# Two transformer blocks on one core: rotary key projected four column groups at a time, low-rank RMS factors moved into later steps, modulation chunks placed elsewhere

## The reference

```python
q = rms_norm(rms_norm(a_q, q_a_norm) @ w_uq, q_norm)        # 256 -> 16 heads x 96
ckv = rms_norm(a_kv[..., :128], kv_a_norm); k_pe = a_kv[..., 128:]     # 32 rotary columns
k_nope, v = split(ckv @ w_ukv)                              # per head 64 + 64
k = rms_norm(concat([k_nope, k_pe]), k_norm)                # k_pe shared by the heads
# rotary on the last 32 of q and k (k of the tokens only), softmax(q k / sqrt(96)) v, @ w_o
```

## Time and profile before

| | us |
|---|---|
| median of 3 runs | 3618.05 (3613.52 to 3625.37) |
| the profiled execution | 3612.44 |
| its span on the core | 3610.6 |
| TensorE busy (matmuls) | 3333.5 (92%) |
| VectorE, ScalarE, GpSimd busy | 1522.1, 1336.0, 1319.5 |

### The profile page before, as it was taken

How to read it: one execution, slowest core, us unless ns; L and a number is a source line. 1 busy time by engine, 2 the same in 40 slices (tenths; PEclk the granted TensorE clock), 3 DMA queues, 4 the chain that set the end, 5 groups by cost and what they waited for, 6 DMA issues and landing times.

```text
span 3610.6 us, 40889 instructions
## 1 busy us (share of the span) xinstructions
PE 3333.5 (92%) x16580; PEld 2671.7 (74%) x16580; DVE 1522.1 (42%) x2662; ACT 1336.0 (37%) x2305; POOL 1319.5 (37%) x731
## 2 busy tenths in 40 slices
PE   7988899999967989999989998989998989889998
PEld 4854788888854667788877687868887667768886
DVE  5557332222245776321233546253223455734232
ACT  4222332222323565332333534343333453434243
POOL 2224432222320000544462047444455124564446
PEclk9999999999978999999999999999999999999999
DMA  5145112112104200123222120322322212022322
GB/s 222 59 157 200 47 55 72 56 62 65 58 5 167 74 13 1 70 88 105 85 100 90 41 83 1 108 77 85 108 88 94 70 47 75 6 84 94 105 85 67
DMA packets 85639, 286.11 MB, mean 79 GB/s; under 512 B 9771, under 2 KB 10347, under 8 KB 84940
## 3 DMA queue, kind: packets, MB, share of 16 engines
q1 hardware_dynamic: 85452, 283.50, 23.3%
HBM read 281.37 MB, written 2.10 MB: 79 GB/s over the span
## 4 chain that ended last, share of the span: by engine, by line
PE 81%; DVE 12%; ACT 4%; DMA 1%; issue 1%; POOL 0%; SPq 0%; DVEq 0%; ACTq 0%
PE ps L443 19%; PE ps L446 19%; PE ps L444 19%; PE ps L468 2%; PE ps L470 2%; PE ps L469 2%; PE ps L1847 2%; DMA ring<-in_w_mod 1%; PE ps L1786 1%; DVE T L2397 1%; PE ps L500 1%; DVE T L616 1%; PE ps L1119 1%; DVE sm L1792 1%; PE ps L1820 1%
## 5 line engine op out<-in xcount | busy, mean ns | idle before, releaser
L388 POOL TENSOR_TENSOR WL<-ring,WH 128x1024 fp32r<-128x1024 f32 (+2 forms) x444 | 960.5, 2167 | 1587.0 <-ACT WH L379 1586.4
L443 PE MATMUL ps<-HX,WH 128*128 128x512 f32 x1832 | 719.0, 392 | 3.5 <-POOL WL L388 3.5
L446 PE MATMUL ps<-HX,WL 128*128 128x512 f32 x1832 | 716.2, 391 | 0.0
L444 PE MATMUL ps<-HX,WH 128*128 128x512 f32 x1832 | 714.7, 390 | 0.0
L379 ACT CAST WH<-ring 128x1024 fp32r<-128x1024 f32 (+2 forms) x444 | 420.7, 949 | 450.1 <-PE ps L446 327.6
L443 PEld LDWEIGHTS ps<-HX,WH 128*128 128x128 f32 x1832 | 344.0, 188 | 83.7 <-issue 5.7
L443 PE MATMUL ps<-FR,WH 128*128 128x512 f32 (+1 forms) x1072 | 400.0, 373 | 0.0
L444 PE MATMUL ps<-FR,WH 128*128 128x512 f32 (+1 forms) x1072 | 390.9, 372 | 0.0
L446 PEld LDWEIGHTS ps<-HX,WL 128*128 128x128 f32 x1832 | 345.3, 188 | 51.9
L444 PEld LDWEIGHTS ps<-HX,WH 128*128 128x128 f32 x1832 | 344.3, 188 | 51.1
L446 PE MATMUL ps<-FR,WL 128*128 128x512 f32 (+1 forms) x1072 | 370.6, 372 | 0.0
(11 more groups left out here) (334 smaller groups left out, 5391.5 us busy)
## 6 DMA issues: line engine op xcount, KB each, us to landing
ring<-in_w_mod SPq DMA_DIRECT2D x96, 512.0 KB, 6.1
ring<-in_ffn_w_up SPq DMA_DIRECT2D x88, 512.0 KB, 3.4
ring<-in_w_up SPq DMA_DIRECT2D x88, 512.0 KB, 3.4
ring<-in_w_in_tok SPq DMA_DIRECT2D x40, 512.0 KB, 3.5
ring<-in_w_in_feat SPq DMA_DIRECT2D x32, 512.0 KB, 3.4
ring<-in_ffn_w_down SPq DMA_DIRECT2D x32, 384.0 KB, 3.1
ring<-in_w_out SPq DMA_DIRECT2D x32, 384.0 KB, 3.1
ring<-in_w_down SPq DMA_DIRECT2D x32, 384.0 KB, 3.1
```

The costliest lines, as they stand in the source:

```text
L388: pool.tensor_tensor(WL[:, p % SPLITS, 0:n], ring.ap(r), WH[:, p % SPLITS, 0:n], ALU.subtract).then_inc(*ring.frees(r, split.g, "low", p))
L443: pe.matmul(o, high, xh, k == 0, False)
L444: pe.matmul(o, high, xl, False, False)
L446: m = pe.matmul(PS[bs[i]][:, 0:N], low, get(k)[0], False, k == g.kt - 1)
```

## The change

- **Key.** The key's weights are no longer split. 32 float32 matmuls (weights 32 columns, activations' high and low part as float32, 512 or 256 streamed) write four column groups; ScalarE copies the two banks, six small matmuls with `pick`, now 128 x 32, add the groups and turn them.
- **Low-rank factors.** The gains are applied as ScalarE evicts the low-rank tiles; their squares are summed by one-column matmuls. RMS of q's low-rank part drops out of the head norm but for its eps, which becomes eps times (mean square + eps), a value per token (`epsq`). The reciprocal root of ckv's (`rkv`) is the scale of the key and value evictions. Heads start after the evictions ("low"); the table and the key and value evictions wait for `rkv` ("small").
- **Chunks.** The mixer steps ten (4 to 9, 12 to 15), one less after the transposes and one less between the inverse transforms. Chunks 10 and 11 run in gap n1, 16 and 17 in n2, 22 and 23 in n3, right after the sums; 18 to 21 in the making of head group 0, every third step; none in attention. `PLACE` gives the order for the two row buffers. In the diff `rows_pe` is the eight matmuls of a chunk, `turned_pe` its four with `pick[:, 0:2]`, both as before; `some_a` copies each row by ScalarE once it is complete; VectorE's one addition for both chunks (`some_v`) stands after all its parts.

```diff
+        def some_pe(pe, c0, n):
+            b = bank.take("mod_n", c0)
+            pe.wait_ge(*bank.free("mod_n", c0))
+            for c in range(c0, c0 + n):
+                rows_pe(pe, c)
+                if c > c0:
+                    turned_pe(pe, c - 1, b, 8 * (c - 1 - c0))
+            turned_pe(pe, c, b, 8 * (c - c0))
...
+        def norm_a(act, name, sts, c0, n):
             for q in sts:
                 root_a(act, q.name, q.N, q.r)
+            some_a(act, c0, n, [nm.pe.at("total", q.name) for q in sts])
             parts_a(act, name, sts)
...
+            r = ring.raw(dr["mla_w_kpe"], 256)
+            for i, (N, parts) in enumerate(((S, HX), (SC, HC))):
+                for half in range(2):
+                    for x in range(2):
+                        for j in range(4):
+                            k = 4 * half + j
+                            m = pe.matmul(PS[bs[i]][32 * j:32 * j + 32, 0:N], ring.ap(r)[:, k * 32:k * 32 + 32], parts[:, k, x, :].bitcast(F32),
+                                          half == 0 and x == 0, half == 1 and x == 1)
...
+            for t in range(4):
+                for k in range(2):
+                    pe.matmul(PS[b][:, t:t + 1], sq[:, k, t * 128:t * 128 + 128], ones[:, 0:1], k == 0, k == 1)
             for t in range(6):
+                m = pe.matmul(PS[b][:, 4 + t:5 + t], sq[:, 2 + t // 4, t % 4 * 128:t % 4 * 128 + 128], ones[:, 0:1], True, True)
...
+            for t in range(6):
+                m = pe.matmul(PS[b][:, t * 32:t * 32 + 32], KP[:, t * 128:t * 128 + 128], pick[:, :], True, True)
...
+                    act.activation(sq[:, g.key + s, 0:N], o, ACT.Square).then_inc(*mla.a.up())
+                    act.activation(dst, o, ACT.Identity, scale=gain).then_inc(*bank.emptied((L_a.name, g.key, s), mla.a))
...
+            dve.tensor_scalar(rkv, ps("stat")[:, 4:10], 1.0 / 128, EPS, ALU.mult, ALU.add).then_inc(*mla.v.up("mean kv"))
+            dve.tensor_scalar(epsq, ps("stat")[:, 0:4], EPS / 256, EPS * EPS, ALU.mult, ALU.add).then_inc(
+                *bank.emptied(("stat",), mla.v))
...
+                dve.scalar_tensor_tensor(by_tile, by_tile, 1.0 / w, eps_of, ALU.mult, ALU.add).then_inc(
...
-            pe.wait_ge(*nm.v.at("small"))
+            pe.wait_ge(*mla.a.at("low"))
...
-                act.copy(ktok[:, t, :].rearrange("p (h c) -> p h c", h=4)[:, :, 0:64], kv[:, :, 0:64]).then_inc(
-                    *mla.a.up())
+                act.wait_ge(*mla.v.at("small"))
+                act.activation(ktok[:, t, :].rearrange("p (h c) -> p h c", h=4)[:, :, 0:64], kv[:, :, 0:64], ACT.Identity,
+                               scale=rkv[:, t:t + 1]).then_inc(*mla.a.up())
...
             for x, _ in enumerate(heads(0)):
-                if x % 4 == 2:
+                if x % 3 == 2:
                     next(last_mod, None)
+            last_of(last_mod)
...
             totals_pe(pe, ["n1x", "n1c"])
+            some_pe(pe, 10, 2)
...
-                        sp.wait_ge(*nm.v.at("small"))
+                        sp.wait_ge(*mla.v.at("small"))
```

More of the change, by code:

```diff
@@ L349, in program @@
         L_ffn0 = ffn_plan("ffn0", "ffn_w_up", "ffn_w_down", 0, 2)
[L350 removed]
+        L_a = Linear(ring, "mla_a").rows(dr["mla_w_a"], 0, 3, 8)
         L_o = Linear(ring, "mla_o").rows(dr["mla_w_o"], 0, 8, 8)
@@ L473, in token_pe, with row_of, rows_pe @@
                     next(beside, None)
+        PLACE = {c: i for i, c in enumerate((*range(0, 10), 12, 13, 14, 15, 10, 11, *range(16, 24)))}
+        def row_of(c):
+            return T[:, 6 + PLACE[c] % 2, :]
+        def rows_pe(pe, c):
+            b = bank.take("mod", c)
+            pe.wait_ge(*bank.free("mod", c))
+            for q in range(4):
+                r = ring.raw(dr["w_mod"][c // 12][c % 12][q], 1024)
+                pe.wait_ge(*ring.landed(r))
+                for j in range(2):
+                    k = 2 * q + j
+                    o = PS[b][32 * (k % 4):32 * (k % 4) + 32, :]
+                    m = pe.matmul(o, cs[:, k, :], ring.ap(r)[:, j * 512:j * 512 + 512], k < 4, k >= 4)
+                m.then_inc(*ring.frees(r, mod.pe, "row", c, q))
@@ L543, in scales_v @@
                                          ALU.add, ALU.mult).then_inc(*nm.v.up())
[L545 to L560, removed]
         def first_sums_a(act, name, src, N, r):
@@ L1550, in ready @@
                 return parts_done("n2", sts, s)
-            linear_pe(pe, L_a, lambda g: [(halves[s], (S, SC)[s], ready(s)) for s in range(1 + (g.key == 2))],
-                      groups=L_a.groups[0:3], front=2)
-            g = L_a.groups[3]
-            p = ring.next()
-            pe.wait_ge(*split.g.at("low", p))
-            b = bank.take("kpe")
-            pe.wait_ge(*bank.free("kpe"))
-            for t in range(6):
-                for k in range(8):
-                    src = (HX, HC)[t // 4]
-                    tt = slice((t % 4) * 128, (t % 4) * 128 + 128)
-                    c = slice(k * 32, k * 32 + 32)
-                    o = PS[b][:, t * 32:t * 32 + 32]
-                    pe.matmul(o, src[:, k, 0, tt], WH[:, p % SPLITS, c], k == 0, False)
-                    pe.matmul(o, src[:, k, 0, tt], WL[:, p % SPLITS, c], False, False)
-                    m = pe.matmul(o, src[:, k, 1, tt], WH[:, p % SPLITS, c], False, k == 7)
@@ new lines, in low_rank_a @@
+                    act.activation(dst, o, ACT.Identity, scale=gain).then_inc(*bank.emptied((L_a.name, g.key, s), mla.a))
+                mla.a.mark("low")
+            act.wait_ge(*mla.pe.at("kpe rows"))
+            for i, N in enumerate((S, SC)):
+                act.copy(KP[:, i * S:i * S + N], ps("kpe", i)[:, 0:N]).then_inc(*bank.emptied(("kpe", i), mla.a))
+            mla.a.mark("kpe")
+            cast_to(act, g.last + 3)
+            act.wait_ge(*mla.v.at("mean kv"))
+            act.activation(rkv, rkv, ACT.Sqrt).then_inc(*mla.a.up("root kv"))
```

186 lines of the change are left out of this document (89 added, 97 removed).

## The result

The changed kernel takes 3569.5 us (median of four runs, 3564.5 to 3573.6) against 3617.4 of the kernel before beside it: ratio 0.9864, 95% interval 0.9841 to 0.9887. Measured a second time, the same kernel gave 0.9884 (0.9864 to 0.9905) with a median of 3575.5. The forecast was 3560, within 3540 to 3582. The profiled execution took 3566.0 us (span 3564.2), 46.4 less than the profiled one before; the sum had said 54.4.

A forecast was written before the change was run, and what follows sets the result against it. TensorE, busy 92% of the span, bounds the kernel. Terms -37.6 - 0.5 + 0.4 + 0.5 - 15.0 + 5.7 - 5.9 - 2.0 = -54.4 give 3558.0 profiled, 3563.6 on the median; forecast 3560 us, range 3540 to 3582.

The forecast's parts named there:

- Low-rank stage: Rotary key and low-rank norms up to the first query matmul: 16.0 us instead of 53.6, gain 37.6 (31 to 39).
- Rival (a): Key matmuls in four column groups don't overlap: 21.4 us instead of 6.5, 3573 on the profiled execution; chance 10%.
- Warmer query matmuls: First query matmuls, 7.38 us before, may be less cold after a shorter idle: 0.5 us gained (0 to 2).
- Evictions: Key and value evictions become scaled activations, 0.12 us more each: +0.4 in head group 0, +0.5 in groups 1 to 3.
- Mixer: Two of twelve chunks leave the mixer: 7.6 us gained at its front, 7.4 at its end, together -15.0.
- The three gaps: Two chunks in each norm gap; late ring slots and ScalarE's row copy delay the modulated parts: +5.7 us (2 to 14).
- The flight: Late chunk transfers in the gaps: a 512 KB transfer lands 3.4 us after issue, the two behind it 1.3 us each.
- rival (b): Late gap transfers take 6.1 us instead of 3.4, 2.7 more in each gap: +8, 3566; chance 15%.
- Attention 0: Four chunks leave the first attention, 85.9 us before and 80.0 without them: gain 5.9 (5 to 7).
- Transposes: The last chunk's rows leave the transposes that end the latent stage: 2.0 us gained (1 to 3.4).
- Rival (c): Work in the gaps keeps TensorE's clock at the high level: 6.5 us more gained, 3551; chance 15%.
- (d): Slower than before: nothing prefetched in the gaps, eight transfers in a row, 40 us per gap, 3672; chance 3%.

The follow-up runs named there:

- chunks_only: Kernel before plus the chunk moves alone, with its old low-rank stage and evictions: 3612.0 us beside 3612.9 of the kernel before.
- lowrank_only: Kernel before plus the low-rank part alone, chunks where they stood before: 3575.0 us beside 3612.9 of the kernel before.
- rope_later: Changed kernel with the rotary table's transfer issued behind the first head group's weights instead of ahead of them: ratio 0.9857 to the kernel before.
- key_split: Changed kernel with the rotary key computed as before (144 matmuls on high and low halves), the RMS folding kept: 3597.6 us, ratio 0.9955 to the kernel before.
- key_serial: Changed kernel with the 32 key matmuls ordered one column group after another instead of in turn: key 11.6 us at full clock instead of 5.3.
- after_again: Changed kernel run once more, unaltered, beside the follow-up runs on the same chip: ratio 0.9884 to the kernel before, median 3575.5 us.
- cap: Changed kernel with the next stage's third weight split named after the eight chunk transfers in the three gaps: 3564.8 us, ratio 0.9854 to the kernel before.
- late_turn: Changed kernel with the second chunk's row copied after all modulated parts and turned after the next stage's first pair: ratio 0.9870 to the kernel before.
- key_wide: Changed kernel with key matmuls in serial order and 128 weight columns each, key not computed, trace only: both halves take 20.6 us.
- best2: Changed kernel with late_turn, rope_later, cap in first and third gap only, and chunk 14's addition after two channels: 3561.3 us, ratio 0.9850 to the kernel before.

## Why the prediction was right, and where it was wrong

The total was right: 3560 forecast, 3569.5 and 3575.5 measured. Of its two parts, measured apart, only the low-rank one was. For the chunk moves the terms of the sum were -15.0 + 5.7 - 5.9 - 2.0 = -17.2, and chunks_only measures a ratio of 0.9992, which is -3 us (-7 to +1). That the total stayed in its range is in part luck: the range was wide enough to hold this miss.

- **Low-rank stage: right.** -37.6 forecast, -39.5 in the trace, -38 by lowrank_only. Key 5.3 (6.5 forecast: the 256-column half took 1.84, half of the other, so its weight loads don't pace it), statistics and turn 4.7 (4.7), the wait that ends the stage 4.2 (0.9 for the chain and 3.9 for the flight; 0.5 and 3.7 measured), and rope_later shows that this wait is SyncE's order. TensorEngine Tiling (Array Packing) of the Trainium skill, section Theoretical Speedup, allows up to four times for 32 columns. Against the wide matmul the runs have 3.8 and 3.7, but the packing alone makes only a factor of 2.2 (11.6 to 5.3), the narrow weights the rest. About half of what the key gained is the lower level that its 144 matmuls ran at (see key_split).
- **Rival (a): fell, and its price was wrong.** It priced matmuls that don't overlap at 21.4 us; key_serial measured 11.6. That step took L1119 as the price of a serial narrow matmul, though it differs in two things, width and order. With 11.6 (a) would have given 3563, well inside the range, so the total could not have told it.
- **Warmer query matmuls: -0.5 forecast, not shown.** From the first query matmul to the first key/value matmul the first trace has 6.76 us instead of 7.22, but after_again, the same kernel, has 8.17, and the twelve traces with the short idle have a mean of 7.23 (6.67 to 8.28). That the first trace met the term is luck.
- **Evictions: right.** 0.47 each for 0.38, less than the 0.50 taken. From the key/value matmuls to the transposes +1.4 in all, 1.2 of it VectorE's wait for chunk 18's turn: there the step that held the waits for rows 19 and 20 to be within 0.2 us failed. What made it late is the clock: the last quarter of the rows took 1.73 us and the turn 1.87, at the lower level. In rope_later that quarter lands 20.2 us after the first query matmul, no sooner than here (19.9), but quarter and turn take 1.05 each, and VectorE does not wait. So it is in all traces: a wait of 1.2 to 1.9 us in the six with both at the lower level, 0.6 in after_again with only the rows there, none in the five others with the chunk order of the change.
- **Mixer: right by the traces' means.** -7.5 at the front and -7.8 at the end where -7.6 and -7.4 stood, though the whole stretch fell by 13.1 only in the first trace. Over the twelve traces with the moved chunks it has a mean of 150.5, against 164.0 and 167.0 in the two without, which is the forecast 15.0, give or take the 3 us between these two. Missed: the stall of up to 2.6 us at the bank which chunk 14's addition frees; the addition is no longer covered by a second chunk.
- **The three gaps: the term that was mis-sized.** +1.3, +1.6, +2.8 forecast, +3.4, +3.7, +4.2 measured: 11.3 instead of 5.7 (10.9 in the mean of the eight traces with the changed kernel's gaps), inside the range of 2 to 14 and no gap over 5. The mechanism was the one named: late slots, and ScalarE's copy ahead of all parts. The forecast took off 0.8 for a TensorE that starts less cold, which no idle time shows, so like for like 6.5 stands against 11.3. Mis-sized were two steps. The flight: the step had a 512 KB transfer land 3.4 us after its issue and the two behind it at 1.3 us each; in the first gap they took 3.5, 4.9 and 7.3 from the first issue, so the last was 1.3 us late. The step from that landing to the first part: 1.0 by the sum, for rows and copy, 1.6 measured (425.00 to 426.59). In the third gap the last transfer was late by 0.4 us only (8.5 after the sums, 8.2 forecast), and the second step was the larger; in the second gap the last rows also ran at a granted clock of 0.60. In size 5.6 us is two thirds of the way to rival (b). That the six transfers right behind are what delayed the last one, against (b)'s "those come behind", fits but is not shown: no run holds them back by themselves. cap and late_turn each took a part of the gaps' growth back.
- **Attention 0: -5.9, right.** Transposes -2.0: -1.3 in the first trace, from the first of them to the first score matmul; over the twelve traces with the moved chunks -0.9 against the mean of the two without.
- **Rival (c): fell, but for 0.9 us.** The first matmul after gap 1 does take 0.47 instead of 0.77, but 1.6 us later the lower level comes anyway, and the stretches behind gaps 1 and 2 got shorter by 0.2 and nothing. Behind gap 3 the first 6 us have a granted clock of 0.74 instead of 0.56, and the way to TensorE's next long wait takes 375.9 us instead of 376.8. That 1.1 in all is about the 0.8 that the forecast had taken off, and far from the rival's 4. **(d) fell**: transfers were prefetched.

So the sum missed by 8.0, of which 5.6 lie in the idle time of the gaps and 1.9 in the output stage's stall; in the first trace 1.9 too little in the mixer and 1.9 too much in the low-rank stage cancel. What the chunk moves are worth end to end is less than their stretches say: by the means -15.0 + 0.9 (output stage) + 10.9 - 5.9 = -9, but -3 (-7 to +1) in chunks_only, and -9 and -1 as the difference between the whole and lowrank_only. Low clock in attention may account for part of it: eight of the twelve traces with moved chunks have some in attention 0 and 1 (1.3 to 8.3 us), neither of the two without. Whether the four chunks in attention 0 kept the clock up, or this is chance, stays open: it needs more profiled executions of both.

## What to carry to other kernels

Before filling an idle gap, list every buffer slot, queue and in-order engine that the filling passes through: a gap in TensorE is full of work of the engines that end it, and one late transfer ahead of their first instruction moves it all. Send narrow float32 matmuls to different column groups in turn; here that made a factor of two, and the narrow weights another. Look at the granted clock before you take busy time for work. When terms fall below the scatter of the clock, judge them by their stretch in the trace, in more than one trace, and don't book the sum of the stretches as time won: the chunk moves shortened the mixer by 15 us and chunks_only as a whole by nothing that can be measured.

## What the runs showed of the hardware

- A float32 matmul of 512 columns takes 0.87 us with 128 weight columns (key_wide), 0.44 with 32 in one column group (key_serial), and 0.23 with 32 and the groups in turn (the changed kernel); at 256 columns 0.44, 0.28 and 0.12.
- 144 matmuls of 128x32 hold TensorE busy without a pause at a granted clock of 0.56 (0.55 in the kernel before): they begin at the 2.4 GHz level, 0.11 us apart, and fall to the 1.2 GHz level while TensorE stays busy, 0.21 apart. A busy TensorE is not one at its higher level.
- VectorE's additions on 128x512 take 1.64 to 1.86 us instead of 0.69 to 0.74 while GpSimd works beside them (the changed kernel from 338.86, best2 from 346.26). GPSIMD Engine Reference of the Trainium skill, section Architecture, says that the two share the read and the write port; the rows fit that.
- A stall of 2.55 us in a dense stretch was followed by 5.9 us at the lower clock level (cap, 344.1 to 350.0), which cost the stage another 3 us. The stall of 1.69 us at the same place in the changed kernel was followed by a granted clock of 1.00 (345.98 to 350.0).
